# Moving operands of the split products 32 bytes lower in SBUF

## What is computed

```python
p = h @ w_in_l                                    # 256x1024 by 1024x2576
return (jax.nn.silu(gate) * val) @ w_down_l       # 256x2816 by 2816x1024
proj = h @ w_in                                   # 256x1024 by 1024x11272
f = jnp.square(jax.nn.relu(h @ w1)) @ w2          # 256x1024x4096, 256x4096x1024
```

## The kernel before

| Buffer | Start | Start modulo 256 |
|---|---|---|
| raw (4 slots), w_hi, w_lo (2 each) | 16512, 49280, 65664 | 128 |
| x | 82048 | 128 |
| F: act_hi0, act_hi1, act_lo0, act_lo1 | 90432, 98624, 106816, 115008 | 64 |
| R: ada_raw, s7, s8, vtok_r | 123264 | 128 |
| consts_common, consts_stage | 141696, 143744 | 128 |
| small_weights | 160224 | 224 |
| silu_c_wide, strip_rows | 164544, 165568 | 192 |
| std, rstd, smalls | 166688, 167712, 168736 | 32 |
| A: seven tiles of 8192 | 170304 and up | 64 |

## Time and profile before

### The profile page before, as it was taken

One profiled execution on the slowest core, in us unless ns is written; L12 is line 12 of the kernel. 1 busy time (PEld: TensorE's weight loads), 2 busy tenths in 40 slices (PEclk: granted clock), 3 DMA queues, 4 the chain that ended last, 5 costly groups with the idle time before them and its releaser, 6 DMA issues.

```text
span 2107.0 us, 35267 instructions
## 1 busy us (share of the span) xinstructions
PE 1885.6 (89%) x15156; PEld 1776.3 (84%) x15156; DVE 1191.0 (57%) x1499; ACT 798.7 (38%) x966; POOL 34.3 (2%) x68
## 2 busy tenths in 40 slices
PE   6988898988799798999988699998999989789998
PEld 4777797867698697999888689996999989788997
DVE  2464656553588636455756755456344566757453
ACT  2343100003433334444465434444335455534342
POOL 0010000010000000000000000000000000000000
PEclk7997899999899899999999899999999999899999
DMA  9576404064344253544443325553444444343552
GB/s 394 198 268 232 160 1 160 27 223 151 119 161 158 102 184 126 182 148 151 150 153 138 140 100 177 186 177 112 168 141 160 141 154 166 108 144 128 182 185 93
DMA packets 45206, 329.27 MB, mean 156 GB/s; under 512 B 5008, under 2 KB 5008, under 8 KB 5392
## 3 DMA queue, kind: packets, MB, share of 16 engines
q1 hardware_dynamic: 35712, 258.63, 34.7%
q0 software_dynamic: 9216, 67.11, 8.4%
q10 hardware_dynamic: 144, 1.51, 0.2%
HBM read 326.18 MB, written 1.05 MB: 155 GB/s over the span
## 4 chain that ended last, share of the span: by engine, by line
PE 64%; DVE 15%; ACT 8%; issue 7%; DMA 5%; DVEq 0%; SPq 0%; ACTq 0%; POOL 0%
PE ps L324 16%; PE ps L326 15%; PE ps L325 15%; ACT w_hi L896 4%; DMA ada_raw<-ada 4%; DVE w_lo L1336 3%; PE ps L583 3%; PE ps L595 2%; DVE gacc L1726 2%; PE ps L438 2%; PE ps L593 2%; PE ps L417 2%; DMA ada<-ada 1%; DVE rstd L1374 1%; DVE rsq L2002 1%
## 5 line engine op out<-in xcount | busy, mean ns | idle before, releaser
L324 PE MATMUL ps<-act_hi,w_hi 128*128 128x256 f32 x2672 | 769.5, 288 | 82.7 <-DVE act_lo L1369 58.8
L1336 DVE TENSOR_TENSOR w_lo<-raw,w_hi 128x2048 fp32r<-128x2048 f32 x211 | 483.2, 2292 | 596.5 <-ACT w_hi L896 595.6
L325 PE MATMUL ps<-act_lo,w_hi 128*128 128x256 f32 x2672 | 756.8, 283 | 0.0
L326 PE MATMUL ps<-act_hi,w_lo 128*128 128x256 f32 x2672 | 756.2, 283 | 0.0
L896 ACT ACTIVATE w_hi<-raw 128x2048 fp32r<-128x2048 f32 (+1 forms) x233 | 428.6, 1841 | 603.0 <-PE ps L326 602.7
L324 PEld LDWEIGHTS ps<-act_hi,w_hi 128*128 128x128 f32 x2672 | 517.5, 194 | 93.2 <-issue 62.7
L325 PEld LDWEIGHTS ps<-act_lo,w_hi 128*128 128x128 f32 x2672 | 518.0, 194 | 0.9
L326 PEld LDWEIGHTS ps<-act_hi,w_lo 128*128 128x128 f32 x2672 | 517.7, 194 | 0.0
L324 PE MATMUL ps<-mlp_hi,w_hi 128*128 128x256 f32 x512 | 144.7, 283 | 8.5 <-DVE mlp_lo L2005 8.5
L325 PE MATMUL ps<-mlp_lo,w_hi 128*128 128x256 f32 x512 | 143.1, 280 | 0.0
L326 PE MATMUL ps<-mlp_hi,w_lo 128*128 128x256 f32 x512 | 143.1, 279 | 0.0
(11 more groups left out here) (385 smaller groups left out, 2527.1 us busy)
## 6 DMA issues: line engine op xcount, KB each, us to landing
raw<-stream SPq DMA_DIRECT2D x233, 1024.0 KB, 4.8
ada_raw<-ada POOLq DMA_DIRECT2D x64, 1024.0 KB, 6.7
ada_f<-ada SPq DMA_DIRECT2D x4, 1024.0 KB, 14.2
ada_a<-ada SPq DMA_DIRECT2D x3, 1024.0 KB, 19.8
consts_stage<-consts_a SPq DMA_DIRECT2D x1, 1728.0 KB, 32.8
consts_stage<-consts_b ACTq DMA_DIRECT2D x1, 1472.0 KB, 7.5
x<-xT SPq DMA_DIRECT2D x1, 1024.0 KB, 7.2
xc<-ctxT SPq DMA_DIRECT2D x1, 1024.0 KB, 9.2
```

The lines of the kernel that those rows point to most:

```text
L324: mm(out, ah, bh, start=first, stop=False, skip_group_check=shared)
L325: mm(out, ah, bl, start=False, stop=False, skip_group_check=shared)
L326: return mm(out, al, bh, start=False, stop=last, skip_group_check=shared)
L1336: tt(w_lo[:, s2, :], raw[:, s4, :], w_hi[:, s2, :].bitcast(f32), ALU.subtract).then_inc(S("lo_ready"), 1)
```

## The change

It takes 32 bytes from the gap ahead of F and puts them behind it, and makes the gap ahead of A end at 32 modulo 256 in place of 64 (`place[0]` is 170272 there, so the gap becomes 0 bytes in place of 32).

```diff
         x = new("x", [P, KT, T])
-        room(192)
+        room(160)
         F = [room(8192) for _ in range(4)]
-        room(64)
+        room(96)
         act_hi = [at(f"act_hi{i}", [P, KT, T], F[i], f32r) for i in range(2)]
         act_lo = [at(f"act_lo{i}", [P, KT, T], F[2 + i], f32r) for i in range(2)]
         R = [room(8192), room(8192)]
@@
         sm = new("smalls", [P, 12, 32])
-        room((64 - place[0]) % 256)
+        room((32 - place[0]) % 256)
         A = [room(8192) for _ in range(7)]
         assert (A[0] - F[0]) % 256 == 0
```

## The result

| | before | after |
|---|---|---|
| median of 4 runs, us | 2093.68 | 2130.53 |
| lowest, highest | 2089.4, 2108.97 | 2123.99, 2131.72 |
| profiled execution, its span | 2108.82, 2107.0 | 2130.94, 2129.1 |
| granted TensorE clock over the span | 0.941 | 0.947 |

The changed kernel is slower: the ratio of the times, taken from the means of the runs, is 1.0156, with an interval of 1.0101 to 1.0211, or 33 us. (The two medians are 37 us apart.) The granted clock is no lower than before. The two programs issue the same instructions in the same order on every engine.

A forecast was written before the change was run, and what follows sets the result against it. TensorE was taken to bound the kernel, through its split products. Matmuls, VectorE and ScalarE work, and DMA each summed to 0 change, giving the median of before, 2093 us, with a range of 2066 to 2138 us.

The forecast's parts named there:

- slow pace everywhere: Split products: every restart falls into the 117.8 ns pace, 22 to 28 us more, 2115 to 2121 us; chance 0.11.
- third pace: Split products: moving read begins inside a 64-byte block, one 4.4 ns step each, 45 us, 2128 to 2138 us; chance 0.20.
- no effect: Whole kernel: the change costs 0 apart from paces dealt anew, some ±10 us; 2093 us, chance 0.43.
- What bounds the kernel: Whole span: TensorE busy 89% of 2107.0 us, split products 969 us of the chain, 0.78 of their work on the path.
- The distance between starts as the price: TensorE streams without a stop: a matmul costs the distance between starts, 113.3 or 117.8 ns, not its duration of 276 to 288.
- Term 1: Matmuls: 10,080 get a moving operand 32 bytes lower, taken as 0 change.
- the sixteen narrow matmuls at 224: Fourier stage, 128 columns, operand at 32 modulo 64: 111 ns each, read as showing that such an address costs nothing.
- the exchange of addresses: Feature against token chunks: moving and weight addresses 64 and 128 swap, both orders show both paces, so it moves nothing.
- The addresses do not choose the pace: Split products: the pace, 113.3 or 117.8 ns, is chosen when the stream restarts and then kept, whatever the operand addresses.
- Fast everywhere: Split products: 32 bytes less lifts a collision of moving and weight reads, 13 us less, 2080 us; chance 0.10.
- the floor of the weight load: Split products: every one goes at 111.7 ns, 26 us less, 2067 us; chance 0.16 for this or lower.
- Terms 2 and 3: VectorE and ScalarE on moved tiles, and DMA: each taken as 0, allowing perhaps 2 us on the path and 2 us.

The follow-up runs named there:

- the widths: TensorE alone, computation left out, 128 to 512 moving columns at eight address differences: 111.6 to 111.7 ns at 128 columns, 226.7 to 234.3 at 512.
- the sweep: TensorE alone, computation left out, 12 streams of 48 split matmuls at each of sixteen address differences in 16-byte steps, weights at 128: 113.3 to 120.0 ns.
- difference 0: Whole kernel before, with moving operands put at 128 modulo 256 like the weights: 2141.15 us beside 2099.97, ratio 1.0191.
- the 64 differences: TensorE alone, computation left out, address differences 0 to 252 in steps of 4 bytes, 5 streams each: 113.3 ns at 112 and 192, others between 116 and 123.

## Why the prediction was right or wrong

The time lies inside the range, above "slow pace everywhere" (2115 to 2121) and within the third pace's 2128 to 2138. The forecast itself, no effect, was wrong, and so was the mechanism behind it. That the range holds the time is owed to a rival whose price came out near for a wrong reason. (In that rival two steps, counted as one was, would be 2163 to 2183, not 2173.)

- **What bounds the kernel.** Right. The loss is TensorE's, and it shows in the chain as TensorE's share. That 0.78 of the products are on the path was near enough: the two profiled executions give 22.1 / 33 = 0.67, the means of the runs 1.
- **The distance between starts as the price.** Right, and the whole study rests on it. Durations of single matmuls hardly tell it: 288 ns before, 290 after for 2,672 at L324, while the distance rose 3.2.
- **Term 1, the matmuls, taken at 0.** This is the step that failed. Measured: 3.2 ns on each of 10,300, 33 us. Its first support was the sixteen narrow matmuls at 224. They were the nearest in address and could not show it: at 128 columns the pace is 111.7 at every difference, as the widths show. I had written that they were bound by the weight load, and the conclusion should have been that they are no evidence. Its second support was the exchange of addresses between feature and token chunks. It compares -64 with +64, and among the multiples of 32 these two are the only ones that have 113.3 at all. Nor did it move nothing: before, 190 of 748 distances in token chunks were fast and some 6,330 of 9,430 in the others. The last sentence of the prediction named that gap, that -64 and +64 can be alike where -96 is not, and this is what happened, though not modulo 128 (96 gave 120.0 and 224 gave 118.4); it was given no chance of its own.
- **"The addresses do not choose the pace."** Half right. The difference sets which paces there are; at 64 and 192 there are two, and within the sweep the wait ahead of the stream repeated its choice. How it picks is open. "Kept, across chunks and across tiles" was read from 924 to 950 us alone: at 883.1 us the same trace goes from 117.8 to 113.3 without a stop, at the border of a token and a feature chunk.
- **The third pace.** Nearest of the rivals, but its mechanism, a read that begins inside a 64-byte block, is refuted by the kernel with both operands 32 lower (both old paces back) and by difference 0 (aligned, and slowest). Its price of 4.4 ns on each was near for what had been fast (113.3 to 117.3 or 118.7) and too much for what had been slow (117.8 to the same values), so 45 us became 33.
- **Slow pace everywhere.** Its size, 22 to 28 us, is just under what came. It failed on the token chunks (120.0, not 117.8) and on the stretches at 118.7 to 120.
- **Fast everywhere, the floor of the weight load.** Neither came. The floor of 111.7 is real, for up to 192 columns; with 256 no address gave less than 113.3, and the trace's 111.7 for narrow matmuls was no bound that a product could reach. The figure of the Trainium skill, "TensorE: Matmul & The Clock Gate", section "Back-to-back issue gap", N/2.4 + 2.5 or 109.2 ns, was reached at none of the 64 differences; the best measured is 4.1 ns above it and the worst 14. In the same section the Trainium skill gives that figure for an isolated matmul; for a stream with a weight load each it has about 81 ns at 128 columns and 131 at 512, and the widths gave 111.7 and at best 226.7.
- **Terms 2 and 3.** Right at 0: 2,292 ns and 1,915 ns, 426 and 419, 4.8 us per transfer.

The Trainium skill says in the same page, in the section "Step-by-step: what each phase is for", that TensorE has two independent SBUF read ports and that a weight load takes no read bandwidth from the running matmul. No run here shows what the ports do, but a pace that hangs on the two addresses together, with no other engine at work, does not fit two reads that know nothing of each other.

## What to carry to other kernels

Before an SBUF layout is changed, write down for each kind of matmul the start of the moving operand less that of the stationary one, modulo 256, and measure the distance between starts in a stretch that never stops, since the difference alone does not give the pace; in a kernel bound by 256-column float32r products a change of that difference by 32 bytes was worth 1.6%. A row of the trace is evidence on a cost only if the operation in it could have shown that cost: a matmul bound by its weight load can't show what the moving read costs. Two arrangements that show the same values (-64 and +64) don't prove that the arrangement has no part in it; ask which quantity they share.

## What was unexpected of the hardware

- The distance of back-to-back float32r matmuls of 256 columns, each with its own weight tile, at the granted clock of 1.00 (the 2.4 GHz level), hangs on both start addresses, and turns within a running stream when they do: 113.3 ns at best, 120.0 at equal addresses, up to 123 at single 4-byte steps.
- At the differences 64 and 192 two paces, 113.3 and 117.8 ns, exist at the same addresses. The stream falls into one within some ten matmuls and stays there while the difference does; in the first sweep the same wait ahead of it gave the same pace both times; with weights at 16 modulo 32 and difference 192 only the fast one was seen, in 32 of 32 streams.
- The same holds for wide ones: 512 columns took 226.7 ns at difference 0 and 234.3 at 160; 320 columns took 146.7 at all eight. From 320 columns on each took at least 13.3 ns more than its columns.
- 128 and 192 columns both take 111.7 ns with a weight tile each, at all eight differences, and plain float32 matmuls of 256 columns did not react to the change (215.8 and 215.9 ns).
- Open: the cause inside the chip, how the start picks between the two paces, what beside the two addresses modulo 256 counts, and why the kernel with both operands 32 lower is 11 us slower where its distances explain 5.
